# Storing the last half tile of gates by 32 tokens each, in a hybrid attention, gMLP and PEER block

## The reference

```python
q = (x @ w_query).reshape(T, PEER_HEADS, 2, PEER_HALF)
s1, s2 = scores of both halves against 128 keys each
v1, i1 = lax.top_k(s1, 16); v2, i2 = lax.top_k(s2, 16)
sc, flat = lax.top_k(v1[..., :, None] + v2[..., None, :], 16)
e = i1[flat // 16] * 128 + i2[flat % 16]        # expert numbers, 16384 experts
g = softmax(sc)
u = expert_u[e]
a = gelu(einsum('cd,chkd->chk', x, u))
out = einsum('chk,chkd->cd', g * a, expert_v[e])
```

## Time and profile before

| | us |
|---|---|
| median of 3 runs (1651.46 to 1656.78) | 1652.03 |
| the profiled execution, whole | 1650.74 |
| its span | 1649.0 |
| PE busy / DVE busy / ACT busy / POOL busy, in the span | 1514.5 / 1359.4 / 660.5 / 817.4 |
| the chain that ended last: PE / DVE / DMA / issue / POOL | 78% / 12% / 4% / 3% / 2% |
| of it, DMA w_scratch<-staged | 3% |

### The profile page before, as it was taken

The page is one execution under the profiler, slowest core; times in us unless marked ns, Lnnn a source line. Parts: engine busy times, 40 slices in busy tenths (PEclk is TensorE's granted clock), DMA queues, the critical chain, the costliest instruction groups (busy, mean ns, idle before and its releaser), DMA issues.

```text
span 1649.0 us, 25530 instructions
## 1 busy us (share of the span) xinstructions
PE 1514.5 (92%) x7943; PEld 1297.0 (79%) x7943; DVE 1359.4 (82%) x2696; ACT 660.5 (40%) x1105; POOL 817.4 (50%) x799
## 2 busy tenths in 40 slices
PE   5999999999967548869999999999999999999996
PEld 3677766776656537759999999999999999999995
DVE  5676634342989999869999999999999999999997
ACT  4332445422156644424334333343343443443433
POOL 1000000001059867657666666666666666666662
PEclk8999999999979759989999999999999999999998
DMA  9974211340000419999999999999999999999992
GB/s 348 373 277 157 89 51 52 128 182 1 1 1 1 103 43 262 249 361 406 407 385 384 387 381 383 382 390 381 383 387 383 385 382 387 379 392 381 383 385 98
DMA packets 226331, 448.90 MB, mean 272 GB/s; under 512 B 96779, under 2 KB 113443, under 8 KB 226028
## 3 DMA queue, kind: packets, MB, share of 16 engines
q1 hardware_dynamic: 170092, 243.65, 42.5%
q0 software_dynamic: 56192, 204.66, 31.7%
HBM read 424.44 MB, written 23.10 MB: 271 GB/s over the span
## 4 chain that ended last, share of the span: by engine, by line
PE 78%; DVE 12%; DMA 4%; issue 3%; POOL 2%; ACT 1%; SPq 0%; DVEq 0%; POOLq 0%; ACTq 0%
PE bank L831 14%; PE bank L1008 9%; PE bank L1009 9%; PE bank L1007 9%; PE bank L1030 7%; PE bank L1028 7%; PE bank L1029 7%; PE bank L768 4%; PE bank L1020 4%; PE bank L1021 3%; DMA w_scratch<-staged 3%; PE bank L934 2%; POOL hot L703 1%; PE bank L901 1%; DVE halves L1739 1%
## 5 line engine op out<-in xcount | busy, mean ns | idle before, releaser
L1007 PE MATMUL bank<-h_hi,u_hi 128*128 128x320 f32 x1024 | 316.4, 309 | 3.3 <-DVE u_lo L1819 3.3
L1008 PE MATMUL bank<-h_lo,u_hi 128*128 128x320 f32 x1024 | 317.1, 310 | 0.0
L1009 PE MATMUL bank<-h_hi,u_lo 128*128 128x320 f32 x1024 | 317.0, 310 | 0.0
L679 POOL DMA_INDIRECT v_rows<-v_exp,small x192 | 259.5, 1352 | 91.5 <-POOL small L675 51.8
L679 POOL DMA_INDIRECT u_rows<-u_exp,small x192 | 242.7, 1264 | 92.5 <-POOL small L675 52.1
L1342 ACT ACTIVATE v_hi<-v_raw 128x1024 fp32r<-128x1024 f32 x128 | 135.8, 1061 | 246.0 <-PE bank L1030 246.0
L1030 PE MATMUL bank<-v_hi,g_both 128*128 128x512 f32 x512 | 205.0, 400 | 0.0
L1028 PE MATMUL bank<-v_hi,g_both 128*128 128x512 f32 x512 | 204.2, 399 | 0.0
L1029 PE MATMUL bank<-v_lo,g_both 128*128 128x512 f32 x512 | 203.9, 398 | 0.0
L1007 PEld LDWEIGHTS bank<-h_hi,u_hi 128*128 128x128 f32 x1024 | 192.7, 188 | 8.7 <-issue 3.4
L1008 PEld LDWEIGHTS bank<-h_lo,u_hi 128*128 128x128 f32 x1024 | 192.8, 188 | 6.8
(11 more groups left out here) (247 smaller groups left out, 2931.0 us busy)
## 6 DMA issues: line engine op xcount, KB each, us to landing
u_raw<-u_by_key SPq DMA_DIRECT2D x128, 512.0 KB, 6.3
v_raw<-v_exp SPq DMA_DIRECT2D x128, 512.0 KB, 8.4
ada_blk<-ada_w SPq DMA_DIRECT2D x22, 1024.0 KB, 10.2
w_scratch<-staged SPq DMA_DIRECT2D x5, 4096.0 KB, 22.1
w_row<-w_scratch SPq DMA_DIRECT2D x124, 160.0 KB, 9.6
ring<-w_in SPq DMA_DIRECT2D x18, 1024.0 KB, 5.1
xr<-x SPq DMA_DIRECT2D x8, 512.0 KB, 6.2
ring<-w_branch SPq DMA_DIRECT2D x4, 1024.0 KB, 5.1
```

Source lines behind the costliest of these rows:

```text
L679: pool.indirect_dma_start(out=rows[:, s], out_offset=None, in_=table, in_offset=bass.IndirectOffsetOnAxis(ap=ix[:, s:s + 1], axis=0))\
L1007: pe.matmul(o, u_hi[:, r, k], h2_hi[:, k], start=(k == 0), stop=False)
L1008: pe.matmul(o, u_hi[:, r, k], h2_lo[:, k], start=False, stop=False)
L1009: last = pe.matmul(o, u_lo[:, r, k], h2_hi[:, k], start=False, stop=(k == KD - 1))
```

## The change

The half tile is stored by two stores of 32 tokens each in place of one of 64. The first stands ahead of the wait for all groups and ahead of the copy to `w_row`, and itself waits for 64 + 32/4 = 72 groups; the second stands where the one store stood. Both count to `split_stored`, and the three who wait for it (SP, POOL, DVE) wait for 32 in place of 16.

```diff
             for q in range(STEP):
                 sp.dma_start(w_row[:, q, 0:DS - EX], w_dram[:, q, 0:DS - EX]).then_inc(w_row_in[q], 16)
+            store_gates(SPLIT, 0, EX // 2, split_stored)
             sp.wait_ge(w_staged, ALL_GROUPS)
             sp.dma_start(w_row[:, :, DS - EX:DS], staged[SPLIT][:, 0:STEP, :]).then_inc(first_gates, 16)
-            store_gates(SPLIT, 0, EX, split_stored)
+            store_gates(SPLIT, EX // 2, EX, split_stored)
...
                 if q == 1:
-                    sp.wait_ge(split_stored, 16)
+                    sp.wait_ge(split_stored, 32)
                     load_gates(0, STEP)
...
             pool.wait_ge(first_gates, 16)
-            pool.wait_ge(split_stored, 16)
+            pool.wait_ge(split_stored, 32)
...
-            dve.wait_ge(split_stored, 16)
+            dve.wait_ge(split_stored, 32)
             two = ident.rearrange("p (t a) -> p t a", a=2)
```

## The result

The changed kernel takes 1659.46 us in the median of 13 runs (1657.61 to 1661.93), the kernel before in the same sessions 1651.29 us (13 runs). The ratio is 1.0045, with a 95% interval of 1.0037 to 1.0052: slower by 7.4 us (6.1 to 8.6), where +19.3 was forecast. The sign, the place and the chain were right, the size was not. (1659.46 us lies within the stated range of 1657 to 1676, but only because a rival had set its low end.)

The account below looks back on a forecast made before the run. The landing of `split_stored` was taken to bound the kernel. 0 (start) + 19.3 (16,384 more packets at 1.177 ns) + 0 (first gates, refills, covered) on 1652.0 gave 1671.3 us, range 1657 to 1676.

Parts of the forecast that it names:

- What bounds the kernel: Ahead of 738 us, three transfers in a row set the end; `split_stored` landing later costs microsecond for microsecond.
- No early start: First half's issue on SP: about 684.45 us in place of 685.14, behind four `w_row` loads; 0 us, at most -0.7.
- The cost of a packet: Half tile's store: 16,384 more packets at 1.177 ns each, whatever their length; +19.3 us.
- its sign of being wrong: Second half's store taking 10 to 14 us would show the forecast wrong and a rival on bytes right.
- The 32-byte row: Load of c: 132 packets in 250 ns, one in 1.9 ns; read as smaller packets not raising the packet rate.
- The bounds named for this unknown cost: Cost of 128-byte packets in the two halves: +0 by bytes alone, +19.3 us by packets; +26.4 if dearer.
- The rival of a fixed part and bytes: Halves' packets cost a fixed part plus their bytes, 0.81 ns each: +7.2 us, 1659 us; chance 0.20.
- overhead of 3 cycles: Per packet, on top of one cycle per 32 bytes: 11 cycles for 256 bytes, 7 for 128; halves +5.3 us.
- The stall beside the gathers: 693 to 700 us: six `u_rows` gathers make the store 5 us late; as before, now falling on the first half.
- The late first gates: `first_gates` copy queued behind the first half, landing about 712 us, 21 us late; covered by the second half, 0 us.
- The dearer short writes: Each half lands as slowly as the contended store, 26.35 us: +26.4 us, 1678 us; chance 0.08.

Follow-up runs that it names:

- the quarters: Against the kernel before: the half tile stored by four stores of 16 tokens (64-byte runs), behind the copy to `w_row`; 1.0185, +30.5 us.
- the order alone: Against the kernel before: still one store of 64 tokens, but moved ahead of the wait for all groups and the copy to `w_row`; 1.0021, +3.5 us.
- The cut alone: Against the kernel before: copy to `w_row` first, as before, then two stores of 32 tokens in place of one of 64; 1.0050, +8.3 us.

## Why the prediction was wrong, step by step

- **What bounds the kernel** held. The landing of `split_stored` set the end: +7.1 us there, +7.6 at block 3, +7.4 in the runs.
- **No early start** held: 686.86, behind the four loads. The move ahead of that wait, tried by itself, brought 3.0 us at the landing and nothing in the times that is clear of their spread.
- **The cost of a packet is the step that failed.** The forecast took 1.177 ns, read from 256-byte packets, as the pace of packets of any length, and charged 16,384 more of them: +19.3. There is a pace of packets, but it is 0.74 ns, from 32 to 128 bytes; 256-byte packets lie above it. So 32,768 x 0.737 = 24.1 us stand against 19.3: +4.9 in place of +19.3. The second half's packets took 16,384 x 0.737 = 12.1 us, within the 10 to 14 that the forecast had named as its sign of being wrong (14.49 with start and receipt). The 32-byte row was given more than it could bear: it is a load, with 132 packets and the engines 27% busy, and what spaced them by 1.9 ns no row shows. The bounds named for this unknown cost, +0 and +19.3, did hold the truth; choosing the upper one as the value was the mistake.
- **The rival of a fixed part and bytes** (+7.2, 1659 us) had the time right, but not the reason. Its line would make 64 bytes cheaper than 128, and the quarters show that they aren't. Its 0.81 ns was near 0.737 by luck, and its sum left out the stall beside the gathers, which added 2.2 us. The Trainium skill's overhead of 3 cycles for a packet ("DMA: Bandwidth & Descriptors", section "Why small descriptors are slow (HBM only)") gave an estimate of +5.3, close to the +4.9 of the steady paces; but by it, too, runs of 64 and 32 bytes would come faster than 128, and the steady stretches of the trace don't show that.
- **The stall beside the gathers** was taken as unchanged, and that is the second step that missed. From 4.9 to the measured 7.1 at the landing 2.2 us are missing. The first half held SP's queue until 706.5, 19.6 us from its issue, against 25.0 (684.69 to 709.64) for the one store in the same place in the kernel with the order alone. That is 5.3 us less, where the paces give 7.2 less. So some 2 us fall to the first half beside the gathers. The traces show where. While both queues are full, the store passes one packet for each packet of the gathers, however short its own are; here before (696 to 698 us, 256 bytes) and after (700 to 702 us, 128 bytes):

```profile
q0 software_dynamic: 206, 0.76, 92.5%
q1 hardware_dynamic: 224, 0.06, 12.6%
...
q0 software_dynamic: 216, 0.79, 96.1%
q1 hardware_dynamic: 216, 0.03, 8.8%
```

When the gathers are through, the one store makes part of its delay good and the halves don't; before from 700 to 706 us, after from 704 to 706:

```profile
q1 hardware_dynamic: 6739, 1.73, 126.3%
...
q1 hardware_dynamic: 2794, 0.36, 162.7%
```

Before, 6739 packets pass in 6 us, where 1.177 ns would let 5098 through: 1641 packets, 1.9 us made good. So the forecast's 5 us are better read as what was left of a longer delay. After, it is one in 0.72 ns, hardly faster than the steady 0.737. The six gathers bring 768 rows of 4 KB, each a packet. The 768 packets that the store gets through beside them are 0.9 us of its own work at 1.177 ns, but only 0.6 at 0.737, so the halves lose 0.3 us more there. That and the 1.9 make an estimate of 2.2. The cut alone has 8.5 us at the landing in its trace, 1.4 more than the changed kernel; that part stays open.
- **The late first gates** held as covered, with less to spare than thought: the third `gated` was forecast 17.5 us ahead of `acc` (726.5 and 744.0) and came 12.9 ahead (721.84 and 734.72). The changed kernel (1.0045) and the cut alone (1.0050) cannot be told apart. With one store in the same place the cover was gone, and it cost 3.5 us.
- **The dearer short writes** (+26.4) fall: the packets came closer together when the runs shrank, 0.737 ns against 1.177. The Trainium skill ("DMA: Bandwidth & Descriptors", "Specifications") says that transfers below 512 bytes are read, changed and written back. No run here shows whether they are; the rate was the same with 384 bytes (289 GB/s) as with 512 (290).

## What to carry to other kernels

A store whose runs are short is priced by its packets and by the pace at that very length: take the pace from a row with this run length, or measure it in a store that nobody waits for, before one charges a count. Moving or splitting a transfer gained nothing here, where the wait ahead of it on the issuing queue, or the queue itself, set its start; the gain lay in longer runs for the transfer on the chain. Beside another transfer count packets against packets: a store of short runs got one short packet through for each 4 KB packet of the gathers, and a store of 32 KB runs held the gathers back in the same way. So a transfer that is made faster beside another may only hand its wait to that one.

## What the runs showed of the hardware

- Stores from SBUF to HBM passed one packet in 0.74 ns in their steady stretches with 32, 64 and 128 bytes, 1.18 with 256, 1.33 with 384, 1.76 with 512. Two us early in a store with 32-byte runs showed 0.60 ns.
- Equal packets of 256 bytes ran at 1.18 ns in one stretch and at 0.88 or 0.89 in others, behind the loads of experts and behind the gathers. At that faster pace they move 290 GB/s, the rate of the 384- and 512-byte runs. What sets the slower pace, and why 128 bytes aren't bound to it, is open: no run here parts the cutting up of the transfer from the writing.
- With both queues full, the engines passed as many packets of the one as of the other, whatever their length: 224 of 256 bytes beside 206 of the gathers, 216 of 128 beside 216, 224 of 64 beside 225 (the four quarters, 697 to 699 us), 464 of 4 KB beside 452, and 41 of 32 KB beside 38.
- So a store in runs of 32 KB held back 4 KB gathers on the other queue: 10.4 us of waiting for them in place of 3.0, and 4.05 when the same store was issued in eight with runs of 4 KB.
